# Scores of the two head halves as two 64-row products in one attention kernel on one core

## The reference, cut to what matters

```python
# differential attention: 4 heads, each with two halves of dimension 64
s  = einsum('bhqd,bhkd->bhqk', q, k) * scale + bias     # once for (q1, k1), once for (q2, k2)
w  = softmax(mask(s1)) - lam * softmax(mask(s2))
o  = einsum('bhqk,bhkd->bhqd', w, v)
# stick-breaking attention: 8 heads of dimension 64
z = einsum('bhqd,bhkd->bhqk', q, k) * scale
log_1m  = where(causal, log_sigmoid(-z), 0)
between = reversed_cumsum(log_1m) - log_1m
a = where(causal, exp(log_sigmoid(z) + between), 0)
o = einsum('bhqk,bhkd->bhqd', a, v)
```

## Time and profile before

| | |
|---|---|
| median of 3 runs | 1539.3 us (1535.33 to 1544.74) |
| the profiled execution | 1536.03 us, of it 1534.3 us span |
| PE busy | 1435.3 us, 94% of the span |
| DVE, ACT, POOL busy | 35%, 28%, 3% |
| projection | about 22 to 164 us of the span |
| DA stage | about 164 to 232 us |
| SB stage | about 232 to 298 us |
| experts | about 369 to 872 us |

### The profile page before, as it was taken

One profiled execution on the slowest core, in us unless ns is written; L12 is line 12 of the kernel. 1 busy time (PEld: TensorE's weight loads), 2 busy tenths in 40 slices (PEclk: granted clock), 3 DMA queues, 4 the chain that ended last, 5 costly groups with the idle time before them and its releaser, 6 DMA issues.

```text
span 1534.3 us, 16709 instructions
## 1 busy us (share of the span) xinstructions
PE 1435.3 (94%) x6926; PEld 915.8 (60%) x6926; DVE 530.9 (35%) x967; ACT 430.3 (28%) x727; POOL 41.6 (3%) x87
## 2 busy tenths in 40 slices
PE   6999998896999999998999879999999999999996
PEld 5788556684454445444454353555447888887885
DVE  3322577735211211121121045267344222223233
ACT  5432348722100000000200143156334222223222
POOL 1000002200000000000000021000000000000000
PEclk9999999998999999999999989999999999999999
DMA  7452690144699999999999751200004223222201
GB/s 278 144 156 82 281 421 6 50 170 165 281 427 428 427 426 429 428 398 410 416 398 406 282 196 60 77 29 1 1 0 177 97 110 110 83 82 110 82 0 55
DMA packets 30196, 313.87 MB, mean 205 GB/s; under 512 B 3908, under 2 KB 3908, under 8 KB 12456
## 3 DMA queue, kind: packets, MB, share of 16 engines
q1 hardware_dynamic: 22312, 295.06, 47.0%
q10 hardware_dynamic: 6656, 13.53, 2.8%
q0 software_dynamic: 1152, 4.19, 0.8%
HBM read 298.35 MB, written 14.43 MB: 204 GB/s over the span
## 4 chain that ended last, share of the span: by engine, by line
PE 78%; DMA 13%; DVE 5%; ACT 2%; issue 1%; POOL 1%; SPq 0%; ACTq 0%; DVEq 0%; POOLq 0%
PE ps L55 75%; DMA ring<-in_w 7%; DMA B<-in_w 3%; PE ps L1052 2%; DMA ring<-in_w_ada 1%; DVE LL L1611 1%; DMA X<-in_x 1%; DVE TMP L1750 1%; PE ps L796 0%; DMA B<-yslots,SMI 0%; DVE LH L1753 0%; PE ps L563 0%; DVE X L1614 0%; POOL TMP L499 0%; PE ps L651 0%
## 5 line engine op out<-in xcount | busy, mean ns | idle before, releaser
L55 PE MATMUL ps<-ring,B 128*64 128x512 f32 (+4 forms) x888 | 268.1, 598 | 19.4 <-DMA ring<-in_w 14.1
L55 PEld LDWEIGHTS ps<-ring,B 128*64 128x64 f32 (+1 forms) x888 | 91.1, 149 | 142.8 <-issue 132.6
L55 PE MATMUL ps<-B,B 128*128 128x128 f32 (+2 forms) x1096 | 148.9, 296 | 3.9 <-DVE B L1862 3.9
L55 PEld LDWEIGHTS ps<-B,B 128*128 128x128 f32 (+1 forms) x1096 | 126.7, 191 | 29.8 <-issue 25.1
L55 PE MATMUL ps<-B 128*64 128x512 f32 (+5 forms) x376 | 136.0, 576 | 8.1 <-DMA ring<-in_w 5.2
L55 PE MATMUL ps<-XH,WH 128*128 128x512 f32 (+1 forms) x368 | 140.9, 383 | 1.3 <-DVE XL L1611 0.7
L55 PE MATMUL ps<-XL,WH 128*128 128x512 f32 (+1 forms) x368 | 139.7, 380 | 0.0
L55 PE MATMUL ps<-XH,WL 128*128 128x512 f32 (+1 forms) x368 | 139.7, 380 | 0.0
L1520 ACT ACTIVATE WH<-ring 128x2048 fp32r<-128x2048 f32 x33 | 63.2, 1916 | 167.9 <-PE ps L55 167.9
L1611 DVE TENSOR_TENSOR WL<-ring,WH 128x2048 fp32r<-128x2048 f32 x33 | 75.7, 2293 | 95.1 <-ACT WH L1520 95.1
L1351 ACT ACTIVATE TMP<-ps 64x512 f32<-64x512 f32 x32 | 19.0, 593 | 236.7 <-PE ps L55 236.6
(11 more groups left out here) (290 smaller groups left out, 2016.2 us busy)
## 6 DMA issues: line engine op xcount, KB each, us to landing
ring<-in_w SPq DMA_DIRECT2D x65, 2048.0 KB, 16.6
B<-in_w SPq DMA_DIRECT2D x24, 2048.0 KB, 17.1
ring<-in_w_ada SPq DMA_DIRECT2D x12, 2048.0 KB, 9.6
ring<-in_w_gu SPq DMA_DIRECT2D x11, 2048.0 KB, 8.2
ring<-in_w_in SPq DMA_DIRECT2D x7, 2048.0 KB, 8.9
TO<-in_w SPq DMA_DIRECT2D x7, 2048.0 KB, 17.2
ring<-in_w_down SPq DMA_DIRECT2D x5, 2048.0 KB, 7.3
yslots<-TMP ACTq DMA_DIRECT2D x64, 128.0 KB, 8.7
```

What stands on the lines that cost most here:

```text
L55: return e.matmul(o, l, r, start=first, stop=last, skip_group_check=True)
```

## The change

The four zero-padded tensors become two without padding. `dq` and `sq` hold both halves in 128 rows, like the keys. A score product reads 64 rows of the queries and 64 rows of the keys, rows 0 to 63 for one half or head and rows 64 to 127 for the other, and so takes half of the array's rows. In DA the two halves' products stand next to each other in PE's queue and write to different PSUM banks. In SB all the score products of one head take the same 64 rows, and the next head the other 64. DVE writes a query step with one instruction in place of two, and so does ACT. The only zeros left are those that the DMAs read (`ZERO`, 64 rows by 1024), and the wait for these DMAs moves from ACT's queue to SP's, ahead of the load that overwrites the slot.

```diff
--- before.py
+++ after.py
@@ -163,8 +163,7 @@
     dq, dk, sq, sk = (B3[:, 2048 * m:2048 * m + 2048].rearrange("p (m n) -> p m n", m=4) for m in range(4))
     dv = B1[:, 0:2048].rearrange("p (t n) -> p t n", t=4)
     sv = B1[:, 2048:4096].rearrange("p (t n) -> p t n", t=4)
-    QX = ring[:, 4, :].rearrange("p (s m n) -> p s m n", s=2, m=4)
-    dq1, sq1 = QX[:, 0], QX[:, 1]
+    ZERO = ring[0:64, 4, 0:1024]
     UH, UL = ([again(f"{n}{k}", [128, 1024], "ring", SLOT * 3 + 2048 * k + a) for k in range(2)] for n, a in (("UH", 0), ("UL", 1024)))
     NORM = [[TMP[:, 1024 + 1024 * k + 512 * j:1536 + 1024 * k + 512 * j] for j in range(2)] for k in range(2)]
 
@@ -450,6 +449,7 @@
             e.wait_ge(*consumed(before[i]))
             load(i)
         e.wait_ge(sb_o, 4)
+        e.wait_ge(zero_out, 16 * NOVF)
         load(I_EXP + 1)
         load(I_EXP + 2)
         for i in range(I_EXP + 3, I_EXP + 5):
@@ -492,8 +492,7 @@
 
 
     def gpsimd(e):
-        for z in (dq[64:128], dq1[0:64], sq[64:128], sq1[0:64]):
-            e.memset(z, 0.0).then_inc(zero_set, 1)
+        e.memset(ZERO, 0.0).then_inc(zero_set, 1)
 
         def select(d):
             return e.affine_select(out=d, in_=d, compare_op=ALU.is_gt, fill=0.0, base=0, pattern=[[1, 128]], channel_multiplier=-1)
@@ -584,11 +583,11 @@
             else:
                 hi, lo = (w.rearrange("p (c n) -> p c n", c=8) for w in (hi, lo))
                 if kind in (0, 1) and n >= 3:
-                    e.wait_ge(dqk_out, 2 * (n - 2) if n - 3 < 4 else 8 + n - 6)
+                    e.wait_ge(dqk_out, n - 2)
                 if n == 12:
-                    e.wait_ge(dqk_out, 12)
+                    e.wait_ge(dqk_out, 8)
                 if n >= 15:
-                    e.wait_ge(sq_out, 2 * min(n - 14, 4))
+                    e.wait_ge(sq_out, min(n - 14, 4))
                 if n == 19:
                     e.wait_ge(sk_out, 1)
                 e.wait_ge(proj_lo, n + 1)
@@ -608,8 +607,7 @@
             if h == 0:
                 e.wait_ge(sk_out, 4)
             mm(e, P[h], rev, TBR[h], True, True).then_inc(tb_mm, 1)
-        e.wait_ge(dqk_out, 12)
-        e.wait_ge(zero_set, 4)
+        e.wait_ge(dqk_out, 8)
         for i in range(18):
             if i < 16:
                 qt, h = DA[i]
@@ -619,7 +617,7 @@
                 else:
                     e.wait_ge(da_max, 3 * (i - 2) + 2)
                 for j in range(2):
-                    m = mm(e, P[p + j][:, 0:w], (dq, dq1)[j][:, h, 128 * qt:128 * qt + 128], dk[:, h, 0:w], True, True)
+                    m = mm(e, P[p + j][:, 0:w], dq[64 * j:64 * j + 64, h, 128 * qt:128 * qt + 128], dk[64 * j:64 * j + 64, h, 0:w], True, True)
                 m.then_inc(da_s, 1)
             if i >= 2:
                 qt, h = DA[i - 2]
@@ -678,11 +676,11 @@
             e.wait_ge(sbn_act, 3 * m + 1)
             mm(e, P[6 + m % 2], blk, TO[:, 0:512], True, True).then_inc(sbn_mm, 1)
 
-        e.wait_ge(sq_out, 8)
+        e.wait_ge(sq_out, 4)
         e.wait_ge(sk_out, 4)
         for i in range(10):
             if i < 8:
-                m = i // 2
+                m, r = i // 2, slice(64 * (i % 2), 64 * (i % 2) + 64)
                 for g in (2, 1, 0):
                     if i >= 2:
                         e.wait_ge(sb_exp, 3 * (i - 2) + 3 - g)
@@ -690,7 +688,7 @@
                         e.wait_ge(*((da_max, 48), (da_wt, 16))[i])
                         e.wait_ge(ada_row, 12)
                     for c in blocks[g]:
-                        t = mm(e, place(i, c), sk[:, m, 128 * c:128 * c + 128], (sq, sq1)[i % 2][:, m, 128 * c:512], c < 3, True)
+                        t = mm(e, place(i, c), sk[r, m, 128 * c:128 * c + 128], sq[r, m, 128 * c:512], c < 3, True)
                     t.then_inc(sb_z, 1)
             if 1 <= i < 9:
                 if i == 1:
@@ -1193,13 +1191,13 @@
                 if n == 4:
                     e.wait_ge(zero_set, 1)
                 e.dma_start(ydram[CAP * (NE + n - 4):CAP * (NE + n - 3), :].rearrange("p (m n) -> p m n", m=2),
-                            dq[64:128, 0:2, :]).then_inc(zero_out, 16)
+                            ZERO.rearrange("p (m n) -> p m n", m=2)).then_inc(zero_out, 16)
             if n < 23:
                 proj_high(n + 1)
             if 1 <= n <= 8:
                 j = n - 1
                 if j >= 2:
-                    e.wait_ge(dqk_out, 2 * (j - 1) if j - 2 < 4 else 8 + j - 5)
+                    e.wait_ge(dqk_out, j - 1)
                 e.wait_ge(proj_mm, n)
                 e.activation(NORM[j % 2][0], P[j % 3], ACT.Square).then_inc(dn_act, 1)
                 e.wait_ge(dn_mm, j + 1)
@@ -1208,9 +1206,7 @@
                 rsqrt(NORM[j % 2][1]).then_inc(dn_act, 1)
             if 13 <= n <= 16:
                 e.wait_ge(proj_mm, n)
-                for j, d in enumerate((sq, sq1)):
-                    r = slice(64 * j, 64 * j + 64)
-                    e.activation(d[r, n - 13, :], P[(n - 1) % 3][r, :], ACT.Copy, scale=0.125).then_inc(sq_out, 1)
+                e.activation(sq[:, n - 13, :], P[(n - 1) % 3], ACT.Copy, scale=0.125).then_inc(sq_out, 1)
             if n in (11, 23):
                 e.wait_ge(proj_mm, n + 1)
                 for k in range(4):
@@ -1298,7 +1294,6 @@
             if i in (5, 7, 9):
                 wo_norm((i - 5) // 2)
             if i == 8:
-                e.wait_ge(zero_out, 16 * NOVF)
                 wo_high(0)
                 e.wait_ge(lam_set, 3)
                 for m in range(4):
@@ -1645,8 +1640,7 @@
                 e.wait_ge(dn_act, 3 * j + 3)
                 den = NORM[j % 2][1]
                 if j < 4:
-                    for d, r in ((dq, slice(0, 64)), (dq1, slice(64, 128))):
-                        times(d[r, j, :], P[j % 3][r], qg[r], den[r], ALU.mult).then_inc(dqk_out, 1)
+                    times(dq[:, j, :], P[j % 3], qg, den, ALU.mult).then_inc(dqk_out, 1)
                 else:
                     times(dk[:, j - 4, :], P[j % 3], kg, den, ALU.mult).then_inc(dqk_out, 1)
             if 17 <= n <= 20:
```

## The result

The changed kernel takes 1545.38 us in the median (20 runs, 1539.98 to 1548.52), the kernel before 1538.09 us (20 runs): ratio 1.0039, 95% interval 1.0027 to 1.0051, so 4 to 8 us slower. That is within the 1% that I called "no change" and inside my range, but it is not my +0.1 us. The profiled execution has a span of 1545.1 us against 1534.3. The experiments further down have 9 to 12 runs each, with 20 or 35 of the kernel before beside them.

The account below looks back on a forecast made before the run. In DA, PE and the `w_ada_2` transfers were both full, the last transfer binding; in SB the chain alternated between DVE, ACT and PE. Terms -0.1 - 0.1 + 0.3 = +0.1 us gave a median of 1539.4 us, range 1532.5 to 1545.5.

Parts of the forecast that it names:

- rival C: Start of SB: z(0) and z(1) overlap, PE idles and the clock rises later; +4.5 us, 1543.9; chance 0.05.
- What the score products gain: DA pairs: two 64-row products overlap fully, so the 16 pairs save half, 8.7 us of PE work.
- What the mode costs: DA rounds: 0.10 us to enter 64-row products and 0.10 to leave, 3.2 us over 16 rounds.
- DA up to block 11: DA rounds with transfers: the `w_ada_2` transfers hide PE's saving; gain 0.1 us, ends 0 and 1.
- End of DA and SB stage: Rounds 12 to 15: -0.1 us, ends -0.7 and +0.6; SB's z products: only switches cost, +0.3, ends 0 and +1.8.
- D: SB: the clock stays at 1.2 GHz through the whole stage; +39 us, 1578; chance 0.03.
- What follows SB moves along one to one: After SB: everything starts from SB's end, so it shifts by the same time.
- Edits at nothing: Query writes, memsets and moved waits: covered by PE's 141.28 us projection or ahead of anything that waits; no time.
- A sum: Whole kernel: -0.1 - 0.1 + 0.3 = +0.1 us, with the forecast's own bounds -1.7 and +2.5.
- A, the transfers give way: DA: blocks land sooner than counted, so PE's saving comes through; -5.2 us, 1534.1; chance 0.08.
- B, no overlap: DA pairs: both halves' passes run one after the other, with switches added; +3.0 us, 1542.3; chance 0.08.

Follow-up runs that it names:

- four slots: Blocks of `w_ada_2` in four slots in place of three: on the kernel before (padded) 0.9998, on the DA part of the change (halves) 0.9993.
- SB alone: Only the SB part of the change, z products over 64 rows, on the kernel before with DA's queries still zero-padded: 1.0035.
- filler: Products of constants where PE idles in DA, added to the DA part of the change with four slots: 0.9990, repeated 0.9979.
- the filled versions: The whole change plus products of the other 64 rows beside z (1.0008), or plus full-row products of constants in SB's waits for ACT (1.0020).
- DA alone: Only the DA part of the change, pairs of 64-row products, on the kernel before with SB's queries still zero-padded: 0.9998.
- rows filled: The whole change plus, beside the z products of heads 1 to 5 and 7, an unread product of the other 64 rows: 1.0008.

## Why the prediction was right, and where it was not

"No change by over 1%" was right, and the reason that I gave for the bound holds: nothing in the change is worth 15 us either way. The +0.1 was not: 7.3 us more were measured. That this lies inside the range is in part luck, since the upper end came from rival C, to which I gave 0.05.

- **What the score products gain**: the overlap is full, as I took it from the column tiles. In the DA rounds the pair costs a constant 0.2 us beyond half: 1.06 in place of 0.86, 0.43 in place of 0.22.
- **What the mode costs**: mis-sized. I had 0.10 to enter and 0.10 to leave; leaving costs 0.20, and a whole DA round pays 0.33 to 0.35 us in place of 0.2. With 256 columns little is left (0.09), and a round with 128 columns is longer than before: with four slots the transposes (the "CST,B" rows) of two such rounds start 2.42 us apart with the halves and 2.31 padded.
- **DA up to block 11** (-0.1, ends a gain of 0 and of 1): the transfers do hide the gain. PE's waits for them are 2.6 us and not the 4.6 that I had, since a round saves less (above) and the blocks come 4.9 us apart and not 5.08. The 0.13 us that I called PE's margin is only the time from landing to start; PE had idled 0.45 us there and had none. The stretch came out at +0.7, because the DMA chain begins with block 0's products and these ran at the low clock after 2.19 us of idle, 1.65 us longer. In the profiles with the halves in DA where the clock held there, projection to block 11 was 194.6, 0.9 us under before, though only 0.4 under SB alone, whose DA is padded. Six profiles have the halves in DA and no filler there, all with the idle of 2.19 us; in four the clock fell at block 0 and in two it held, and what decides it stays open. I had said that what block 3 waits for is left alone by the change; it is, but the idle ahead of it grew by 0.66 us because the pair is shorter.
- **End of DA and SB stage** (-0.1 and +0.3, ends of SB 0 and +1.8): this is the step that failed. It measured +5.3 us. I costed a z product by its columns alone and held the clock to depend on how long PE is busy, and so put C and D at 0.08 together; "it kept 1.00 there" was a fact of padded rows. What happened has about the size of C and the reason that I gave for D, the silent rows: the clock is low from about 227 to 237 us (before from 230) and again in most of 268 to 272 and 285 to 292 us. C's own path, that z(0) and z(1) run side by side and PE idles, is not it: PE is done with them 0.5 us sooner, and the clock rises where it did within a microsecond. The finer table divides the 5.3 us: 0.7 and 2.2 are the two falls (the change less the filled versions), 0.3 in front of the output projection goes with the low clock there, 0.9 are the switches between z(5) and z(7) (0.3 and 0.6 that the filled versions have too), and 1.3 lie ahead of z(5). Of these 1.3 DA alone has 0.5, about what four rounds with 128 columns at 0.1 each come to; SB alone has 0.9, which I can't divide between switches and the longer low clock.
- **What follows SB moves along one to one**: not quite. The output projection starts at the low clock in the change and takes 1.4 us more. It does so in four other kernels, DA alone among them (49.63 us), which is no slower than the kernel before (0.9998), so I don't count this loss as the change's for certain.
- **Edits at nothing**: they held. The projection is 141.31 us without a gap as before (141.28), ACT's one step over 128 rows takes 0.58 us in place of two of 0.59, and SP shows no wait for the clearing DMAs ahead of the expert loads.
- **A sum**: the forecast's upper bound adds up to 0 + 0.6 + 1.8 = 2.4 us, not 2.5. It changes nothing.
- **A, the transfers give way**: no. **B, no overlap**: no. **D**: the clock is low for some 11 us of the 60 after 238 (an estimate from the mean of 0.91), not for all.

## What to carry to other kernels

A product over half of the rows costs its columns all the same, so it is worth it only where its partner runs beside it, and with enough columns to pay for the way in and out (here 0.3 us a round: 512 columns gain, 128 lose). Where it stands alone, as in SB, padding it with zeros is better: SB's halves alone cost 5 us (1.0035). Of the 4.5 us that its profile shows up to the output projection, 2.3 are the two falls and about 0.9 switches. Before crediting a shorter PE stage, look at what ends last in it; here a transfer did, and only a slot more for the transfers let 2 us of the gain through. And where half-filled products and waits of a microsecond follow each other, a product of constants that fits into the wait keeps the clock; in DA it gained 2 us up to the output projection, which gave most of them back.

## What the runs showed of the hardware

- The granted clock does not follow PE's busy time. From 238 to 298 us PE was busy 53.1 us in the change and had 0.91, and was busy 48.6 us in the kernel with padded z and had 1.00. Rows of zeros counted as work as well as rows of data did (padded and rows filled, both 1.00 in 268 to 272 and 285 to 292).
- Two 64-row products of 32-bit numbers into two PSUM banks run side by side in full: four passes of 512 columns in 1.13 us against two in 1.12. Around them 0.1 us goes in entering and 0.2 us in leaving.
- A clock that falls has its place: in two executions of the change it was low in 268 to 272 and 285 to 292 us with the same means, 0.57 and 0.52.
